# Pooled products moved into the projection, the first output block spread over the last score steps, and value tiles made before values

## The reference, cut to what matters

```python
h_l = rmsnorm(x_l, norm_g[l]) * (1.0 + sc) + sh
u_l = h_l @ w_in[l]
k_l = mla_keys(u_l[..., OFF_KV:OFF_MLA_G], kv_norm_g[l], w_ukv[l], rope)   # k_nope, k_rope, v; also for the context
# mixer:
hy   = hyena_mix(u[..., OFF_HY:OFF_HY_G], lp) * silu(...)
att  = softmax((q_nope k_nope + q_rope k_rope) * ATTN_SCALE) @ v           # per head, 512 queries, 768 keys
mla  = att * silu(u[..., OFF_MLA_G:OFF_POOL])
pool = pool_mix(u[..., OFF_POOL:OFF_POOL_G], w_pool, pool_scale) * silu(u[..., OFF_POOL_G:])
out_l = concatenate([hy, mla, pool], axis=-1)
x_l = x_l + gt * (out_l @ w_out[l])
return rmsnorm(x_l, final_norm_g)
```

## Time and profile before

| what | before |
|---|---|
| median of three runs | 943.05 us |
| lowest, highest | 942.75, 945.29 us |
| span of the profiled execution | 941.9 us |
| granted TensorE clock, mean over the span | 0.997 |
| TensorE busy | 925.4 us (98%) |
| VectorE busy | 628.4 us (67%) |
| ScalarE busy | 395.0 us (42%) |
| GpSimd busy | 100.3 us (11%) |

### The profile page before, as it was taken

One profiled execution on the slowest core, in us unless ns is written; L12 is line 12 of the kernel. 1 busy time (PEld: TensorE's weight loads), 2 busy tenths in 40 slices (PEclk: granted clock), 3 DMA queues, 4 the chain that ended last, 5 costly groups with the idle time before them and its releaser, 6 DMA issues.

```text
span 941.9 us, 12349 instructions
## 1 busy us (share of the span) xinstructions
PE 925.4 (98%) x4930; PEld 770.6 (82%) x4930; DVE 628.4 (67%) x850; ACT 395.0 (42%) x622; POOL 100.3 (11%) x78
## 2 busy tenths in 40 slices
PE   9999999999999999999999999999999999999996
PEld 6677788888888888888888888889898788888885
DVE  4655897789967699556975853877777862414244
ACT  3755566535324343243233433545546451213124
POOL 1223200300003000000005630000000000202020
PEclk9999999999999999999999999999999999999998
DMA  9999943223232222287782351101010145223314
GB/s 368 421 419 405 340 144 108 86 86 100 69 96 95 66 90 68 69 284 277 293 289 87 103 176 57 56 12 59 10 49 8 50 160 238 89 90 107 117 45 178
DMA packets 29829, 138.14 MB, mean 147 GB/s; under 512 B 3755, under 2 KB 4267, under 8 KB 22732
## 3 DMA queue, kind: packets, MB, share of 16 engines
q1 hardware_dynamic: 29008, 136.64, 40.0%
q10 hardware_dynamic: 764, 0.72, 0.2%
HBM read 132.10 MB, written 4.19 MB: 145 GB/s over the span
## 4 chain that ended last, share of the span: by engine, by line
PE 90%; DVE 4%; ACT 2%; DMA 2%; issue 1%; POOLq 0%; SPq 0%; ACTq 0%; DVEq 0%
PE pp L1900 38%; PE pp L2197 18%; PE pp L1930 17%; PE pp L1822 5%; PE pp L1799 3%; DMA ada_raw<-in_w_ada_dram 2%; PE pp L2160 2%; PE pp L1830 1%; PE pp L2152 1%; PE pp L2151 1%; DVE softmax_stats L1540 1%; DVE pt_lo L1555 1%; ACT U L910 1%; PE pp L1999 0%; PE pp L2184 0%
## 5 line engine op out<-in xcount | busy, mean ns | idle before, releaser
L1900 PE MATMUL pp<-h_hi,w_hi 128*128 128x512 f32 x544 | 213.2, 392 | 0.1
L1900 PE MATMUL pp<-h_hi,w_lo 128*128 128x512 f32 x544 | 211.8, 389 | 0.0
L1900 PE MATMUL pp<-h_lo,w_hi 128*128 128x512 f32 x544 | 211.8, 389 | 0.0
L1257 DVE TENSOR_TENSOR w_lo<-w_raw,w_hi 128x1024 fp32r<-128x1024 f32 x68 | 87.4, 1286 | 81.0 <-ACT w_hi L707 80.9
L707 ACT ACTIVATE w_hi<-w_raw 128x1024 fp32r<-128x1024 f32 x68 | 71.8, 1056 | 151.1 <-PE pp L1900 105.3
L1900 PEld LDWEIGHTS pp<-h_hi,w_hi 128*128 128x128 f32 x544 | 102.2, 188 | 21.6 <-DVE w_lo L1257 0.5
L1900 PEld LDWEIGHTS pp<-h_hi,w_lo 128*128 128x128 f32 x544 | 102.1, 188 | 21.5
L1900 PEld LDWEIGHTS pp<-h_lo,w_hi 128*128 128x128 f32 x544 | 102.2, 188 | 20.6 <-issue 0.2
L2197 PE MATMUL pp<-wo_hi,m_hi 128*128 128x512 f32 x256 | 100.5, 393 | 0.0
L2197 PE MATMUL pp<-wo_hi,m_lo 128*128 128x512 f32 x256 | 99.6, 389 | 0.0
L2197 PE MATMUL pp<-wo_lo,m_hi 128*128 128x512 f32 x256 | 99.6, 389 | 0.0
(11 more groups left out here) (328 smaller groups left out, 1855.8 us busy)
## 6 DMA issues: line engine op xcount, KB each, us to landing
w_raw<-in_wb_dram SPq DMA_DIRECT2D x68, 512.0 KB, 3.6
ada_raw<-in_w_ada_dram SPq DMA_DIRECT2D x15, 2048.0 KB, 12.7
w_gate_raw<-in_w_gate_dram SPq DMA_DIRECT2D x16, 1024.0 KB, 4.8
wo_raw<-in_w_out_dram SPq DMA_DIRECT2D x16, 1024.0 KB, 4.7
wa_raw<-in_wa_dram SPq DMA_DIRECT2D x16, 320.0 KB, 7.4
UG<-in_xT_dram SPq DMA_DIRECT2D x8, 512.0 KB, 9.2
y<-in_x_dram SPq DMA_DIRECT2D x4, 1024.0 KB, 8.7
wh_raw<-in_w_heads_dram SPq DMA_DIRECT2D x4, 768.0 KB, 4.4
```

The lines of the kernel that those rows point to most:

```text
L1257: eng.tensor_tensor(lane(wb_lo, n % KW), lane(wb_raw, n % KW), lane(wb_hi, n % 2), ALU.subtract).then_inc(wb_lo_done, 1)
L1900: mm = eng.matmul(ps[i][:], w, x, start=(kk == 0 and m == 0), stop=(kk == KT - 1 and m == 2))
```

## The change

It has four parts.

1. *Pooled products.* `pooled(g)` on TensorE moves from steps 29 to 32 of attention into the projection's slots n = 64 to 67, between the two half chunks, in banks 4 and 5 instead of 7. VectorE's part (the product with scale and gate) moves to slots 65 to 67 and behind the loop; it now also waits for the gate tile (`ev_done` 31+g). `keys(0, 0)` and `keys(0, 1)` wait for `pool_out`, since they use banks 4 and 5.
2. *Order of the mixed tiles.* A table `MIX = (0, 1, 2, 3, 12, 13, 14, 15, 4, ..., 11)` sets the order in which the mixed tiles are rounded and used, and the host permutes the rows of `w_out` likewise: Hyena, pooling, heads. So `mixed(4..7)` are now the pooling tiles; they are rounded in steps 28 to 31, and `wo_high(1)`, `wo_low(1)` move from behind the loop into steps 30 and 31.
3. *First output block.* The part for the last token tile (0, 0, 3) is cut up: one k in step 28 (behind `turn`), two in step 29, one in step 31 (ahead of `turn`). It writes bank 7 (instead of 3), which is free once `v_lo_done` is 12. Behind the loop `out_part(0, 1, 0)` is made ahead of `values(7)`.
4. *Value tiles.* In step i = 2 of pairs 1 to 3 `value_tiles(p, 0)` stands ahead of `values(2p-1)` and `turn`. Its rounding `v_hi` now waits for `values(2p-1)` (`pv_mm`), which still reads the old `v_hi`.

```diff
+MIX = (0, 1, 2, 3, 12, 13, 14, 15, 4, 5, 6, 7, 8, 9, 10, 11)
+        def out_bank(b, tok):
+            return ps[4 * (b % 2) + tok if tok < 3 else 3 if b % 2 else 7]
 # ScalarE
             def value_tiles(p, b):
                 eng.wait_ge(v_mm, 3 * p + b + 1)
+                if p and b == 0:
+                    eng.wait_ge(pv_mm, 2 * p)
...
-                if 24 <= n < 28:
+                if 24 <= n < 32:
                     mixed(n - 24)
                 if n == 25:
                     wo_high(0)
+                if n == 30:
+                    wo_high(1)
...
-            wo_high(1)
-            for k in range(4, 8):
-                mixed(k)
 # VectorE
             def pooled(g):
                 eng.wait_ge(pool_mm, g + 1)
+                eng.wait_ge(ev_done, 31 + g)
...
+                if n >= 65:
+                    pooled(n - 65)
...
+            pooled(3)
             rope_cos(0)
...
-                if n in (29, 30, 31, 32):
-                    pooled(n - 29)
-                if 24 <= n < 28:
+                if 24 <= n < 32:
                     mixed(n - 24)
                 if n == 26:
                     wo_low(0)
+                if n == 31:
+                    wo_low(1)
 # TensorE, projection
+            def pooled(g):
+                eng.wait_ge(pool_done, g + 1)
+                if g < 2:
+                    eng.wait_ge(root_done, 6)
+                else:
+                    eng.wait_ge(pool_out, g - 1)
+                eng.matmul(ps[4 + g % 2][:], wp[:, g * P:(g + 1) * P], U[:, (T_POOL + g) * L:(T_POOL + g + 1) * L],
+                           start=True, stop=True).then_inc(pool_mm, 1)
...
+                if n >= 64:
+                    pooled(n - 64)
 # TensorE, attention
+                if h == 0:
+                    eng.wait_ge(pool_out, 3 + part)
...
-            def out_part(b, c, tok):
+            def out_part(b, c, tok, ks=range(4)):
                 n = 4 * b + c
                 eng.wait_ge(wo_lo, n + 1)
+                if n == 0 and tok == 3:
+                    eng.wait_ge(v_lo_done, 12)
...
-                if i == 2 and p:
+                if i == 2 and 0 < p < 4:
+                    value_tiles(p, 0)
                     values(2 * p - 1)
                 if i == 6:
                     values(2 * p)
+                if n in (29, 31):
+                    out_part(0, 0, 3, (1, 2) if n == 29 else (3,))
...
                 if n >= 2:
                     turn(n - 2)
-                if n in (29, 30, 31, 32):
-                    pooled(n - 29)
+                if n == 28:
+                    out_part(0, 0, 3, (0,))
...
-                if i == 2:
+                if n == 2:
                     value_tiles(p, 0)
...
-            out_part(0, 0, 3).then_inc(wo_mm, 1)
+            out_part(0, 1, 0)
             values(7)
-            out_chunk(0, 1)
+            for tok in range(1, 4):
+                mm = out_part(0, 1, tok)
+            mm.then_inc(wo_mm, 1)
```

More of the change, by code:

```diff
@@ L926, in mixed @@
                     eng.wait_ge(q_mm, 8)
-                if k == 4:
+                if k == 8:
                     eng.wait_ge(v_mm, 12)
[L929 to L933, removed]
+                if k >= 8:
+                    eng.wait_ge(o_done, k - 7)
+                elif k >= 4:
+                    eng.wait_ge(pool_out, k - 3)
+                eng.activation(m_hi[MIX[k]][:], ug(MIX[k]), ACT.Copy).then_inc(mix_hi, 1)
             def wo_high(n):
@@ L1564, in pooled @@
                 eng.wait_ge(pool_mm, g + 1)
+                eng.wait_ge(ev_done, 31 + g)
                 x = UG[:, (12 + g) * L:(13 + g) * L]
-                eng.scalar_tensor_tensor(out=x, in0=ps[7][:], scalar=par[:, P_PS + g:P_PS + g + 1], in1=x,
+                eng.scalar_tensor_tensor(out=x, in0=ps[4 + g % 2][:], scalar=par[:, P_PS + g:P_PS + g + 1], in1=x,
                                          op0=ALU.mult, op1=ALU.mult).then_inc(pool_out, 1)
@@ L1751, in _ @@
                     queries(2 * p + 3)
-            wo_low(1)
-            for k in range(4, 8):
+            wo_low(2)
+            for k in range(8, 12):
                 mixed(k)
             gate(7)
-            wo_low(2)
-            for k in range(8, 16):
+            for k in range(12, 16):
                 mixed(k)
@@ L2176, in values @@
                 mm.then_inc(pv_mm, 1)
-            def pooled(g):
-                eng.wait_ge(pool_done, g + 1)
-                if g:
-                    eng.wait_ge(pool_out, g)
-                else:
-                    eng.wait_ge(v_lo_done, 12)
-                eng.matmul(ps[7][:], wp[:, g * P:(g + 1) * P], U[:, (T_POOL + g) * L:(T_POOL + g + 1) * L],
-                           start=True, stop=True).then_inc(pool_mm, 1)
-            def out_part(b, c, tok):
+            def out_part(b, c, tok, ks=range(4)):
                 n = 4 * b + c
                 eng.wait_ge(wo_lo, n + 1)
+                if n == 0 and tok == 3:
+                    eng.wait_ge(v_lo_done, 12)
                 hi, lo = wo_high_[n % 2], wo_low_[n % 3]
-                for k in range(4):
+                for k in ks:
                     kk = 4 * c + k
@@ L2194, in out_part @@
                         eng.wait_ge(mix_lo, kk + 1)
-                    x, w = kk * L + tok * P, k * L
-                    for m, (a, v) in enumerate(((m_hi[kk][:, tok * P:(tok + 1) * P], hi), (m_hi[kk][:, tok * P:(tok + 1) * P], lo), (m_lo[:, x:x + P], hi))):
-                        mm = eng.matmul(psum[:, 4 * (b % 2) + tok, :], a, v[:, w:w + L],
+                    x, w, from_ = MIX[kk] * L + tok * P, k * L, m_hi[MIX[kk]][:, tok * P:(tok + 1) * P]
+                    for m, (a, v) in enumerate(((from_, hi), (from_, lo), (m_lo[:, x:x + P], hi))):
+                        mm = eng.matmul(out_bank(b, tok)[:], a, v[:, w:w + L],
                                         start=(kk == 0 and m == 0), stop=(kk == 15 and m == 2))
@@ L2376, in layout @@
         "x": np.ascontiguousarray(f["x"][0]), "gain": f["final_norm_g"].reshape(1, D), "b_gate": b_ada[2 * D:].reshape(1, D),
-        "w_out": np.ascontiguousarray(f["w_out"][0].reshape(4, 4, P, 4, L).transpose(3, 0, 2, 1, 4)).reshape(16, P, 4 * L),
+        "w_out": np.ascontiguousarray(f["w_out"][0].reshape(KT, P, 4, L)[list(MIX)].reshape(4, 4, P, 4, L).transpose(3, 0, 2, 1, 4)).reshape(16, P, 4 * L),
         "tables": tables.astype(f32),
```

9 lines of the change are left out of this document (6 added, 3 removed).

## The result

The changed kernel takes 951.59 us, the median of four runs (950.1 to 952.38), against 943.12 us for the kernel before in the same comparison: a ratio of 1.0079, 95% interval 1.0056 to 1.0102. So it is 0.8% slower. The forecast was 948.2 us: right in sign and mechanism, and too small. Against the first set's median of 951.59 it is 3.4 us short, and that median lies 0.4 above the range's upper end of 951.2. By the ratio (943.05 x 1.0079 = 950.5 us) and by the second set's median (950.66 us) the time lies inside the range and 2.3 to 2.5 us above the forecast.

The account below looks back on a forecast made before the run. The prediction took TensorE, busy 98% of the span, as the bound. Pair 3's +3.4, pairs 1 and 2's +1.7 and 0 elsewhere gave +5.1 us, a forecast of 948.2 us, range 943.9 to 951.2.

Parts of the forecast that it names:

- What bounds the kernel: Whole kernel: TensorE, busy 98% of the span; only its work or its stops can move the time.
- Part 4, pair 3: Step 26 onward: a 3.60 us stop for `k_lo` and later stops, 6.89 against 3.44 us, so +3.4 us.
- the walk behind it: Pair 3 after the `k_lo` stop: stops of 0.42 at `turn(25)`, 1.84 for `v_lo`, 0.71 at output, 0.32 at `values(6)`.
- Pairs 1 and 2: Attention pairs 1 and 2: longer `k_lo` stop plus 0.42 at `turn`, +0.85 us each, +1.7 together.
- The rival value of 0.4 each: Pairs 1 and 2: only 0.4 us each if the second stop, at `turn`, is absorbed; no separate chance given.
- Part 1: Pooled products moved to the projection: equal TensorE work, 0 us, between -0.3 and +0.5.
- The cover worked out for `keys(0, 0)`: After the projection: `keys(0, 0)` starts 5.4 us past its end, covering VectorE's delay; failure would cost 1 to 2 us.
- The clock: Pair 3's long stop: rival that the granted clock falls, +2.8 us taken (+1.5 to +5.6), 951.0 us, chance 0.2.
- The delay is caught up: Pairs 1 to 3: rival that only the wait for `k_lo` counts, +1.0 us, 944.1 us, chance 0.18.
- the edit does what its order suggests: Pairs 1 to 3: rival that value tiles are ready and all stops go, -4.3 us, 938.8 us, chance 0.08.
- The sum: Whole kernel: 3.4 + 1.7 + 0 = +5.1 us, giving 948.2 us, 0.54% more.

Follow-up runs that it names:

- x1: The changed kernel with part 4 undone, so parts 1 to 3 only: 943.14 us, ratio 1.0001 to the kernel before.
- x6: The changed kernel with value tiles ahead of `values` only in pairs 1 and 2, pair 3 in the old order: 948.34 us (one run).
- x5: The kernel before with part 1 alone, the pooled products in the projection's slots 64 to 67: 944.11 us, ratio 1.0016.
- a2: The changed kernel run again unaltered, the second set of five runs: 950.66 us, ratio 1.0078 to the kernel before.
- x7: The changed kernel with four small matmuls of ones put into the long stop of step 26: 948.89 us, ratio 1.0057.
- x2: The kernel before with part 4 alone, value tiles ahead of `values` and `turn` in pairs 1 to 3: 952.92 us, ratio 1.0085.
- y2: y1 plus the second head's query rotation moved later in every pair on ScalarE and VectorE: 938.92 us, ratio 0.9953.
- y1: The changed kernel without part 4, with `wo_high(0)` behind `keys(7, 1)`, `mixed(0)` in step 25, `wo_low(0)` ahead of `low(24)`: 940.46 us, ratio 0.9975.

## Why the prediction was right, and where its size was off

*What bounds the kernel.* Held: TensorE's work did not change, and its stops made the time.

*Part 4, pair 3.* The stop for `k_lo` was forecast as 3.60 from start to start and measured as 732.51 - 728.91 = 3.60; the walk behind it, `turn(25)` 0.42 and `v_lo` 1.84, as 0.40 and 1.88 (0.24 and 1.72 idle), the one ahead of the output piece 0.71 as 0.57. The stop of 1.53 at `turn(27)` went, as forecast. The last one, 0.32 at `values(6)`, came as 0.29: the last scores' matmul starts at 757.14, the next could start at 757.32 and starts at 757.61, behind a `pt_lo` that ends at 757.56. Together 6.74 against 3.44 before, +3.3 where +3.4 was forecast. The stretches give the same: they have +5.56 - 1.58 = +3.98 for part 4 (x1, x6) and -0.67 for the rest of the stretch (x1's 357.35 + 3.44 against 361.46): +3.3.

*Pairs 1 and 2.* +1.7 forecast, +1.65 measured (x6). The rival value of 0.4 each, with the second stop absorbed, is out: `turn` is idle for 0.24 us in each.

*Part 1.* The middle value of 0 was mis-sized within its bounds: +0.2, for the pooled products cost 0.91 us each between the half chunks (x5) and 0.86 in attention. The cover worked out for `keys(0, 0)` held; no wait stands there.

*The clock.* This is the term that made the forecast too small: the sum has it at nothing, and left it to a rival with a chance of 0.2 and +2.8 us. It happened in all four traced executions with 2.5 us idle or more in this stop, and cost 1.58 and 1.57 us in the changed kernel (a2: 737.03 - 729.84 = 7.19), 1.35 in x7 and 2.72 in x2: near the lower of the bounds given, +1.5 and +5.6, in x7 just under it and in x2 close to the 2.8 taken. The idle time of 3.4 us was in the prediction, and so was the fall 2.8 us behind the last matmul at the end of the kernel. From those rows the fall was the likelier case, and the weak step is that I gave it 0.2. The granted clock of 0.50 in the windows above is also what decides on the rule weighed there, that of the Trainium skill (TensorE: Matmul & The Clock Gate, section "What's actually happening"), by which an idle engine falls back to 1.2 GHz: this trace agrees, with 0.74 and 0.50 behind the stop.

*The rivals.* "The delay is caught up" (+1.0) is refuted by every stop behind the first, "the edit does what its order suggests" by the first.

*The sum.* 3.3 + 1.65 + 0.2 + 1.6 = +6.75 us, so 949.8 us from the median of 943.05; three of the nine runs of the changed kernel stand at 949.76 to 950.1. The other six stand 0.9 to 2.8 us above the lowest. In one of them, the profiled one, 2.7 us are late pieces of `w_in`, seen also in x1, x6, x2 and y2, and runs of before reach 950.12 us as well. So what part 4 does makes 949.8; why the medians stand 0.9 and 1.8 us above that is not shown. Whether the changed kernel meets them more often than the others is open, with nine runs; nothing in its list before chunk 64 differs from before.

## What to carry to other kernels

Moving a product ahead of another pays only if its operands are ready there: read when the last remainder of the pair ends on VectorE, and compare it with when TensorE would start, not with when it started in the old order. Add the price of the clock (here 1.4 to 2.7 us) to a stop as long as those behind which it fell here (2.29 us idle and more), and ask first which short instructions of ScalarE and VectorE stand in front of the wanted one; three such moves (y1) took 2.2 us from the stretch, two more (y2) another 1.6.

## What the runs showed of the hardware that I had not expected

The clock fell behind the stop, not in it, where 3.44 us were idle: TensorE resumed at full clock at 732.51 and 729.84, and the fall came about 1.0 and 1.3 us later. With 2.54 us idle it was down at the restart (0.52 in 730 to 731). In x2, with 3.43 us idle, it was down at the restart too, and stayed there for 6 us in place of 3.3. So a stop of the same length cost 1.6 us of clock in one execution and 2.7 in another. Stops of 1.96, 1.74, 1.72 and 1.65 us left the clock full in the executions traced. The two stops between 1.96 and 2.54 come from late pieces of `w_in`: 2.30 us idle in x1 and 2.29 in y2, and the clock fell some 1.2 and 1.5 us behind the restart in both. So in all six traced stops of 2.29 us and more it fell, and in none of 1.96 and less.

The late pieces: `w_raw` lands 3.5 us after its issue in the median of all 68 (the changed kernel's page). In chunks 43 to 54 SyncE issues a 1 MB piece of `w_gate` ahead of each 0.5 MB piece of `w_in`, and in x1's profiled execution ScalarE could start on the piece issued at 458.80 only at 466.91:

```profile
466.91 1.06 ACT L714 ACTIVATE w_hi<-w_raw 128x1024 fp32r<-128x1024 f32 x1 [5.43 <-DMA w_raw<-in_wb_dram]
```

The next matmul waited 2.30 us for it:

```profile
469.35 0.50 PE L1910 MATMUL pp<-h_hi,w_hi 128*128 128x512 f32 x1 [2.30 <-DVE w_lo L1263]
```

```profile
471.00:472.00 1.00, 1.00 (x3) 0.72 (x3) 1.00 (x2) 0.99 (x1) 0.00 (x0) 0.50 0.00 0
```

The clock was 0.66 in the mean of 470 to 475, so a late piece costs its clock too. That the load beside it is the cause was not tried.
